# Router to first expert: order of the gather, the normed rows and the norm weights in a one-core encoder kernel

## The reference, cut to what matters

```python
def rms_norm(x, g):
    y = xf * lax.rsqrt(jnp.mean(xf * xf, axis=-1, keepdims=True) + EPS)
    return (y * g.astype(jnp.float32)).astype(x.dtype)

def moe_swiglu(x, w_router, w_gate, w_up, w_down):       # x = rms_norm(h, odd_norm2)
    logits = (xf @ w_router).astype(jnp.float32)
    top_val, top_idx = lax.top_k(logits, TOP_K)          # 2 of 8
    weights = jax.nn.softmax(top_val, axis=-1)
    ...                                                   # tokens grouped by expert
    def expert_block(args):
        xb, e = args
        return swiglu(xb, w_gate[e], w_up[e], w_down[e])  # 1024 -> 3584 -> 1024
    ...
h = h + moe_swiglu(rms_norm(h, odd_norm2[j]), ...)
```

## Time and profile before

| | before |
|---|---|
| runs, us | 1448.60, 1442.38, 1449.48 (median 1448.6) |
| profiled execution, us | 1445.53 |
| span of the trace, us | 1443.3 |
| TensorE busy | 1408.8 us, 98% of the span |
| VectorE busy | 1156.2 us, 80% |
| ScalarE busy | 974.0 us, 67% |
| share of the chain that ended last | TensorE 93%, VectorE 3%, ScalarE 2% |
| mean granted TensorE clock | 0.993 |

### The profile page before, as it was taken

The page is one execution under the profiler, slowest core; times in us unless marked ns, Lnnn a source line. Parts: engine busy times, 40 slices in busy tenths (PEclk is TensorE's granted clock), DMA queues, the critical chain, the costliest instruction groups (busy, mean ns, idle before and its releaser), DMA issues.

```text
span 1443.3 us, 19744 instructions
## 1 busy us (share of the span) xinstructions
PE 1408.8 (98%) x7232; PEld 1185.4 (82%) x7232; DVE 1156.2 (80%) x1014; ACT 974.0 (67%) x929; POOL 69.5 (5%) x70
## 2 busy tenths in 40 slices
PE   6999999999999999999999999999999999999997
PEld 6997888888977788888888888888888888888885
DVE  5567766664674888988888899889888889888887
ACT  6455645444853577777777777787777777777775
POOL 0000100000000300100000000000010000000000
PEclk9999999999999999999999999999999999999999
DMA  8634456544453899999999999999999999999992
GB/s 260 220 128 146 151 200 201 179 139 140 134 178 151 295 374 383 352 400 388 371 374 400 380 362 403 375 355 404 387 366 384 390 375 369 402 377 356 403 352 74
DMA packets 201942, 435.88 MB, mean 302 GB/s; under 512 B 10959, under 2 KB 41251, under 8 KB 201892
## 3 DMA queue, kind: packets, MB, share of 16 engines
q1 hardware_dynamic: 198836, 424.70, 80.9%
q0 software_dynamic: 3056, 10.50, 2.5%
HBM read 427.30 MB, written 7.88 MB: 302 GB/s over the span
## 4 chain that ended last, share of the span: by engine, by line
PE 93%; DVE 3%; ACT 2%; issue 1%; DMA 0%; POOL 0%; DVEq 0%; POOLq 0%; ACTq 0%
PE ps L1600 26%; PE ps L1602 26%; PE ps L1601 26%; PE ps L1882 5%; PE ps L1884 3%; PE ps L2174 2%; DVE w_lo L1011 1%; ACT xn L563 0%; ACT w_hi L551 0%; PE ps L1725 0%; PE ps L1689 0%; PE ps L2084 0%; PE ps L2196 0%; PE ps L2031 0%; DMA arena<-mem 0%
## 5 line engine op out<-in xcount | busy, mean ns | idle before, releaser
L1488 DVE TENSOR_TENSOR w_lo<-raw,w_hi 128x2048 fp32r<-128x2048 f32 (+1 forms) x221 | 435.9, 1981 | 56.5 <-ACT w_hi L855 55.4
L855 ACT ACTIVATE w_hi<-raw 128x2048 fp32r<-128x2048 f32 (+1 forms) x221 | 367.3, 1669 | 119.3 <-PE ps L1602 119.3
L1600 PE MATMUL ps<-w_hi,xt_both 128*128 128x512 f32 (+2 forms) x1048 | 405.5, 387 | 3.5 <-DVE xt_both L1381 1.7
L1602 PE MATMUL ps<-w_hi,xt_both 128*128 128x512 f32 (+2 forms) x1048 | 400.0, 382 | 0.0
L1601 PE MATMUL ps<-w_lo,xt_both 128*128 128x512 f32 (+2 forms) x1048 | 399.3, 381 | 0.0
L1488 DVE TENSOR_TENSOR w_lo<-arena,w_hi 128x2048 fp32r<-128x2048 f32 x144 | 294.7, 2052 | 27.0 <-ACT w_hi L855 26.8
L855 ACT ACTIVATE w_hi<-arena 128x2048 fp32r<-128x2048 f32 x144 | 248.8, 1728 | 82.4 <-PE ps L1602 82.4
L1600 PEld LDWEIGHTS ps<-w_hi,xt_both 128*128 128x128 f32 x1048 | 197.0, 188 | 41.1 <-issue 4.8
L1602 PEld LDWEIGHTS ps<-w_hi,xt_both 128*128 128x128 f32 x1048 | 196.9, 188 | 37.1
L1601 PEld LDWEIGHTS ps<-w_lo,xt_both 128*128 128x128 f32 x1048 | 197.2, 188 | 34.8
L1600 PE MATMUL ps<-w_hi,hT_hi 128*128 128x512 f32 x560 | 219.2, 392 | 0.0
(11 more groups left out here) (271 smaller groups left out, 1225.0 us busy)
## 6 DMA issues: line engine op xcount, KB each, us to landing
raw<-exp_gate SPq DMA_DIRECT2D x72, 1024.0 KB, 6.4
raw<-exp_up SPq DMA_DIRECT2D x48, 1024.0 KB, 7.9
arena<-exp_down SPq DMA_DIRECT2D x48, 1024.0 KB, 5.9
arena<-exp_up SPq DMA_DIRECT2D x40, 1024.0 KB, 7.2
raw<-exp_down SPq DMA_DIRECT2D x40, 1024.0 KB, 7.1
arena<-exp_gate SPq DMA_DIRECT2D x24, 1024.0 KB, 7.4
raw<-exp_up SPq DMA_DIRECT2D x32, 512.0 KB, 4.9
raw<-even_gate SPq DMA_DIRECT2D x11, 1024.0 KB, 5.3
```

Source lines behind the costliest of these rows:

```text
L855: ins = act.activation(w_hi[:, n % CUT, at:at + src.shape[1]], src, ACT.Copy)
L1488: ins = dve.tensor_tensor(w_lo[:, n % CUT, cols], src, w_hi[:, n % CUT, cols].bitcast(F32), ALU.subtract)
L1600: pe.matmul(dst, a[0], b[0], start=start, stop=False, skip_group_check=shared)
L1602: return pe.matmul(dst, a[1], b[0], start=False, stop=stop, skip_group_check=shared)
```

## The change

Six things change.

1. The gather's eight blocks go to four banks, two to a bank, and each pair has its own semaphore count (`first_gathered` and `gathered`); ScalarE and VectorE follow pair by pair.
2. ScalarE writes the normed rows `xn`, without the weights, ahead of the gather; VectorE's four weighted instructions and the load of the weight row go.
3. The weights are applied in each unit: four instructions of 128x128 with a per-partition factor take the place of one of 128x512, on ScalarE and on VectorE.
4. ScalarE runs a `Silu` of one column ahead of the gathered blocks, and the table load stands with it.
5. Twelve unread products in place of nine, and four more behind the ranks.
6. VectorE: the cut of the last slot ahead of the units' slot 3 (slot 2 of the unit) moves behind the gather, and `low_unit(0, begun, 1 + CUT)` becomes `3 + CUT`, so the cuts of slots 5 and 6 move ahead of the chain of small instructions and the `memset`.

```diff
+        def pair_ps(k):
+            return ps[:, (2, 5, 3, 6)[k // 2], P * (k % 2):P * (k % 2 + 1)]
 # SyncE
-            sp.wait_ge(sgn_ready, 1)
-            next_gain(4)
 # ScalarE
             high_to(S_MOE - 1 + CUT)
+            norm(4, h, range(1))
             act.wait_ge(gap_ready, 1)
             act.activation(r_gap_exp, r_gap, ACT.Exp).then_inc(gap_exp, 1)
+            norm(4, h, range(1, TT))
 
             def gather_high(v, b):
                 act.wait_ge(gathered, v * 2 + (b + 1))
-                act.activation(gx_hi[:, 4 * b:4 * b + 4, :],
-                               ps[:, 2 + b, :].rearrange("p (k t) -> p k t", k=4),
-                               ACT.Copy).then_inc(gx_hi_ready, 1)
...
                 for k in range(4 * b, 4 * b + 4):
                     ins = act.activation(gx_hi[:, k, :], ps[:, 2 + b, P * (k % 4):P * (k % 4 + 1)], ACT.Copy,
                                          scale=gain_of[:, 4 * KD + k:4 * KD + k + 1])
                 ins.then_inc(gx_hi_ready, 1)
...
+            act.activation(stat[:, 0, 0, 0:1], rstd[:, 4 * TT:4 * TT + 1], ACT.Silu)
+            for b in range(2):
+                act.wait_ge(first_gathered, b + 1)
+                gained_high(4 * b)
+                gained_high(4 * b + 1).then_inc(first_hi, 1)
+                act.wait_ge(gathered, b + 1)
+                gained_high(4 * b + 2)
+                gained_high(4 * b + 3).then_inc(gx_hi_ready, 1)
 # VectorE
             def gather_low(v, b):
                 dve.wait_ge(gx_hi_ready, v * 2 + (b + 1))
-                dve.tensor_tensor(gx_lo[:, 4 * b:4 * b + 4, :], ...
+                for k in range(4 * b, 4 * b + 4):
+                    ins = dve.scalar_tensor_tensor(gx_lo[:, k, :], ...
+                ins.then_inc(gx_lo_ready, 1)
...
+            for b in range(2):
+                dve.wait_ge(first_hi, b + 1)
+                gained_low(4 * b)
+                gained_low(4 * b + 1)
+                dve.wait_ge(gx_hi_ready, b + 1)
+                gained_low(4 * b + 2)
+                gained_low(4 * b + 3).then_inc(gx_lo_ready, 1)
             low_to(S_MOE - 1 + CUT)
...
-            norm_gained(4, h)
             begun = [CUT]
-            low_unit(0, begun, 1 + CUT)
+            low_unit(0, begun, 3 + CUT)
 # TensorE
-            for _ in range(9):
+            unread_products(12)
...
+            unread_products(4)
...
-                        ins = pe.matmul(ps[:, 2 + b, P * (k % 4):P * (k % 4 + 1)], h[:, t, P * k:P * (k + 1)],
+                        ins = pe.matmul(pair_ps(k), h[:, t, P * k:P * (k + 1)], pick[:, t, :], ...)
+                    if k % 4 == 1:
+                        ins.then_inc(first_gathered, 1)
```

More of the change, by code:

```diff
@@ L397, in build @@
             sem("kd_exp"), sem("kd_ready"), sem("kd_turned"), sem("kdt_ready"))
+        first_gathered, first_hi = sem("first_gathered"), sem("first_hi")
         state_done, states_ready, at_done, at_ready, o_done, o_squared, o_ms, o_rstd, o_ready = (
@@ L827, in _ @@
             high_to(S_MOE - 1 + CUT)
+            norm(4, h, range(1))
             act.wait_ge(gap_ready, 1)
             act.activation(r_gap_exp, r_gap, ACT.Exp).then_inc(gap_exp, 1)
+            norm(4, h, range(1, TT))
             def gather_high(v, b):
                 act.wait_ge(gathered, v * 2 + (b + 1))
-                act.activation(gx_hi[:, 4 * b:4 * b + 4, :],
-                               ps[:, 2 + b, :].rearrange("p (k t) -> p k t", k=4),
-                               ACT.Copy).then_inc(gx_hi_ready, 1)
-            for b in range(2):
-                act.wait_ge(gathered, b + 1)
                 for k in range(4 * b, 4 * b + 4):
@@ L842, in _, with gained_high @@
                 ins.then_inc(gx_hi_ready, 1)
+            def gained_high(k):
+                return act.activation(gx_hi[:, k, :], pair_ps(k), ACT.Copy,
+                                      scale=gain_of[:, 4 * KD + k:4 * KD + k + 1])
+            act.activation(stat[:, 0, 0, 0:1], rstd[:, 4 * TT:4 * TT + 1], ACT.Silu)
[6 more added lines that the diff above has]
+                gained_high(4 * b + 3).then_inc(gx_hi_ready, 1)
             act.wait_ge(units_ready, 1)
@@ L1036, in norm @@
                                           ).then_inc(xn_ready[t], 1)
[L1038 to L1045, removed]
             def turned_low(i):
@@ L1450, in gather_low @@
                 dve.wait_ge(gx_hi_ready, v * 2 + (b + 1))
[L1451 to L1454, removed]
+                for k in range(4 * b, 4 * b + 4):
+                    ins = dve.scalar_tensor_tensor(gx_lo[:, k, :], ps[:, 2 + b, P * (k % 4):P * (k % 4 + 1)],
+                                                   gain_of[:, 4 * KD + k:4 * KD + k + 1], gx_hi[:, k, :].bitcast(F32),
+                                                   ALU.mult, ALU.subtract)
+                ins.then_inc(gx_lo_ready, 1)
             dve.wait_ge(ranks_done, 2)
@@ L1470, in _, with gained_low @@
             dve.tensor_copy(unit_i[:], unit_f).then_inc(units_ready, 1)
-            low_to(S_MOE - 1 + CUT)
[L1473 to L1479, removed]
+            def gained_low(k):
+                return dve.scalar_tensor_tensor(gx_lo[:, k, :], pair_ps(k),
+                                                gain_of[:, 4 * KD + k:4 * KD + k + 1], gx_hi[:, k, :].bitcast(F32),
+                                                ALU.mult, ALU.subtract)
+            for b in range(2):
[5 more added lines that the diff above has]
+                gained_low(4 * b + 3).then_inc(gx_lo_ready, 1)
+            low_to(S_MOE - 1 + CUT)
             def low_unit(u, done, last):
@@ L1583, in _ @@
                 dve.tensor_tensor(hs, hs, ps[:, q, :], ALU.add).then_inc(h_summed, 1)
-            dve.wait_ge(gain_in, 16 * 2)
+            dve.wait_ge(gain_in, 16)
             for t in range(TT):
@@ L2126, in _, with unread_products @@
             router_products(1, range(4, 8), 3).then_inc(logits_done, 1)
-            for _ in range(9):
-                pe.matmul(ps[:, 4, :], xt_hi[:, 0, 0:P], xt_both[:, 0, :], start=True, stop=True)
+            def unread_products(count):
+                for _ in range(count):
+                    pe.matmul(ps[:, 4, :], xt_hi[:, 0, 0:P], xt_both[:, 0, :], start=True, stop=True)
+            unread_products(12)
             pe.wait_ge(masks_ready, 1)
@@ L2141, in gather @@
                     for t in range(TT):
-                        ins = pe.matmul(ps[:, 2 + b, P * (k % 4):P * (k % 4 + 1)], h[:, t, P * k:P * (k + 1)],
-                                        pick[:, t, :], start=(t == 0), stop=(t == 1))
+                        ins = pe.matmul(pair_ps(k), h[:, t, P * k:P * (k + 1)], pick[:, t, :], start=(t == 0), stop=(t == 1))
+                    if k % 4 == 1:
+                        ins.then_inc(first_gathered, 1)
                 ins.then_inc(gathered, 1)
```

## The result

| | before | after |
|---|---|---|
| median of six runs, us | 1445.82 (1442.38 to 1449.48) | 1455.94 (1452.78 to 1459.21) |
| profiled execution, us | 1445.53 | 1455.89 |
| span, us | 1443.3 | 1453.7 |
| TensorE busy, us | 1408.8 | 1415.1 |

The ratio is 1.0067, with a 95% interval from 1.0052 to 1.0082. The change made the kernel slower: by 10.1 us in the medians, by 9.7 us (7.5 to 11.9) by the ratio. The ratios in this text stand with their intervals and are not quotients of medians; those come out up to some 0.1% higher.

A forecast was written before the change was run, and what follows sets the result against it. TensorE, busy 98% of the span, was taken to bound the kernel, so only its waits count; -2.4 + 5.4 + 1.7 + 3.1 = +7.8 us on a median of 1448.6 gave 1456 us, range 1448 to 1461.

The forecast's parts named there:

- head, last logits to slot 0: Gather to slot 0: pairs of blocks and a gather at the full clock let TensorE start slot 0 2.4 us earlier.
- `memset` behind slot 6: Ahead of slot 4, TensorE waits for the `memset` behind slot 6's cut: 5.4 us later, a pause of 6.0 us.
- clock behind the pause: Behind the pause at slot 4, 3.4 us at half clock cost 1.7 us of work, bounds 0.5 and 2.5.
- seven unit ends: At later units' ends, VectorE's four instructions a bank push the next slot 0's cut: 7 x 0.45 = 3.1 us.
- One side remark: In the head: no wait of TensorE hung on VectorE's 2.73 us of `xn` work except through the `memset`.
- clock up and clock down in the gather: Two cases for the head: clock up wins 2.4 us; clock falling in the gather wins 0.65, chance 15%.
- cost 0.1 us at most: Ahead of the ranks: the twelve unread products end at 476.0, before the masks' `Exp` at 476.38, costing at most 0.1 us.
- slot 0 at 481.8 us: Sign for the head: the first product of slot 0 at 481.8 us, with no clock fall in the gather.
- 5.3 us or less from the gather's start: Sign for the head: slot 0's first product comes 5.3 us or less behind the gather's start.
- The table load: On ScalarE ahead of the gathered blocks: load of 1.28 us with the small `Silu` ends at 479.1, delaying nothing over 0.1 us.
- seven waits of 0.45 us: Sign at the units' starts: seven TensorE waits of about 0.45 us, released by the cut `w_lo` L1499.
- The margin of slot 41: At a unit's end: slot 41's cut moves to 600.63, 0.2 us left before TensorE's slot 41, so it adds nothing.

The follow-up runs named there:

- x1: The changed kernel with 1 + CUT in place of 3 + CUT, so the cuts of slots 5 and 6 stand behind the `memset` again; 1448.98 us.
- x2: The changed kernel with the `memset` alone moved ahead of all cuts, right behind VectorE's low parts of the first unit; 1448.78 us.
- x4: The changed kernel with VectorE alone taking each later-unit bank in one 128x512 instruction, leaving the weights out of the low parts of units 2 to 8; 1453.12 us.
- x6: The changed kernel without the first `low_unit` call: small chain and `memset` right behind slot 2's cut, cuts of slots 3 to 6 behind them; 1447.81 us.
- x8: x7 with nine unread products and none behind the ranks; 1447.77 us.
- x3: The changed kernel with one 128x512 instruction per later-unit bank on ScalarE and VectorE, leaving the norm weights out of units 2 to 8; 1452.33 us.
- x5: The kernel before with 3 + CUT in place of 1 + CUT as its only edit; 1453.39 us.
- x7: x6 with VectorE cutting the next unit's slot 0 ahead of the second gathered bank; 1448.04 us.
- x9: x7 with ScalarE too cutting the next unit's slot 0 ahead of the second gathered bank; 1444.52 us.
- x10: x6 with one instruction a bank again and GpSimd multiplying the norm weights into the normed rows; 1448.41 us.

## Why the prediction was right, and where its sizes were off

| step | predicted, us | measured, us |
|---|---|---|
| head, last logits to slot 0 | -2.4 (-0.65 if the clock falls in the gather) | -0.97; about -2.38 where the clock stayed up (x1, x2, x4, x6); -0.78 with the fall in the gather (x8) |
| `memset` behind slot 6 | +5.4 | +5.37 |
| clock behind the pause | +1.7 (0.5 to 2.5) | +2.2; 1.5 to 2.2 in x3, x4 and x5 |
| seven unit ends | +3.1 (7 x 0.45) | +3.4 (7 x 0.49) |
| sum | +7.8 | +10.1 in the medians |

**The pause** was right in place, cause and size. x5 shows that the one edit suffices, x1 and x2 that it is the `memset`'s place behind the cut and not the work in the chain. One side remark was wrong: that a wait of TensorE hung on VectorE's `xn` work through the `memset`. x1's expectation put it as a pause of 0 without that work, and the step of 0.96 us stayed.

**The head** is the term that was mis-sized: -2.4 against -0.97. I had two cases, clock up and clock down in the gather. The third is the one that happened: the fall came during the unread products themselves. The ranks, for which the masks had been ready since 476.49 (the VectorE instruction L1428 ended then), started behind the twelve at 478.09, 1.6 us late. My sentence that the products "cost 0.1 us at most" assumed the full clock for them. It holds in x1, x2, x4 and x6 (3.0 us for twelve) and fails in the changed kernel, x3, x7, x9 and x10 (4.6 us). So the sign "slot 0 at 481.8 us" did not come (483.61), while 5.3 us or less from the gather's start did (3.49). The table load itself stood as forecast: 478.24 to 479.52, with the `Silu` at 479.53 and no drain between them.

**The clock behind the pause** was low for 6.8 us, not 3.4. Part of it lay inside the pause and cost nothing; from 500.70 to 505.3 us it cost half of 4.6 us. The bound held. x3 lost as much, x4 and x5 1.5 us, since more of the fall lay in their pauses.

**The unit ends** were right in cause (x3, x4) and size. The seven waits of 0.45 us do not stand in the wait list (five of 0.2); the steps show them. The margin of slot 41, which I had called sufficient, was: the products around its start at 607.8 us follow every 0.23 us.

**The sum.** The four terms as measured give 10.0 us. That this is so close to the medians' 10.1 is in part chance, since the head and the clock are those of one execution and the changed kernel's six executions took 1452.8 to 1459.2 us. I forecast 1456 us on the median of three runs, 1448.6; six runs put before at 1445.8. So the forecast time hit 1455.94 by luck, with a difference 2.3 us too small and a base 2.8 us too high. The chances (slower 0.48, same 0.44) were too even for terms that were each read from rows; the measured 0.67% lies beyond the bound of 0.5%.

## What to carry to other kernels

Ahead of moving an instruction behind another on the same engine, write down what the other waits for. Here the `memset` went behind a cut whose buffer is freed by the very engine that waits for the `memset`. A semaphore count that costs 0.06 us to give should be given as early as its meaning allows, and a small chain costs least where its engine is idle (x6). When an engine fed by two others in turn gets more work, look at the order on both: x7 moved VectorE alone and gained nothing, x9 moved ScalarE too and gained some 3 us.

## What the runs showed of the hardware

- Filler products don't hold the clock for certain. Of the nine traces with twelve products ahead of the ranks, five (the changed kernel, x3, x7, x9, x10) had the fall in the products and four (x1, x2, x4, x6) had none there or in the gather; all three traces with nine products (before, x5, x8) had it in the gather or from just ahead of it. From the last logits to slot 0 it took 9.4 us without a fall, 10.8 with the fall in the products, and 11.0 in x8 with the fall in the gather. So few traces don't settle how often the products help, and x7 against x8 (1.0010 and 1.0016, with intervals that overlap) shows no gain from them that is clear of the noise. Three of the four traces without a fall in the head (x1, x2, x4) had one of 10.2 us some 40 us ahead of it.
- Around a pause of 6 us ahead of slot 4 the clock was at 0.50 for 6.8 us in the changed kernel, x3, x4 and x5, and for as long around x10's pause of 4.6 us. The pause's length alone does not set the fall's: the pause of 2.1 us at 430 to 436 us (TensorE waits for VectorE's `states`) came with a fall of 10.2 us in x1, x2 and x4, of 3.4 us in the kernel before, x5 and x8, and with none in the changed kernel, x3, x6 and x7.
- The spread between runs of one program goes in part with the clock: among the changed kernel's six, a span of 1450.6 us at a mean of 0.993 and of 1457.0 at 0.988. 0.005 of 1455 us is 14.5 us more at half clock, 7 us of work, and the spans differ by 6.4. It is not the whole: x1 has spans of 1443.3 and 1447.0 us, both at 0.995.
- GpSimd's products of two arrays (1.25 us for 128x512) and VectorE's subtraction of two arrays did not run side by side in the one place where they met: 8.03 us is 2.29 + 5.00 and 0.7 more. The Trainium skill, "GPSIMD Engine Reference", section "Specifications", says that GpSimd's SBUF interfaces are shared with VectorE, with contention when VectorE's instruction has two SBUF inputs; the cut has two (the weights and `w_hi`), and the trace agrees.
